# A two-layer hybrid decoder trunk on one core: four buffers of the expert stage at addresses of their own

## The reference

```python
def swiglu(h, w1, w3, w2):
    return (jax.nn.silu(h @ w1) * (h @ w3)) @ w2

def moe_swiglu(h, w_router, w1, w3, w2):
    logits = (h @ w_router).astype(jnp.float32)
    top_val, top_idx = lax.top_k(logits, TOP_K)
    probs = jax.nn.softmax(top_val, axis=-1)
    combine = jnp.sum(jax.nn.one_hot(top_idx, N_EXPERTS, dtype=jnp.float32) * probs[..., None], axis=-2)
    out = jnp.zeros_like(h)
    for e in range(N_EXPERTS):
        out = out + combine[..., e:e + 1] * swiglu(h, w1[e], w3[e], w2[e])
    return out
```

## Time and profile before

| quantity | value |
|---|---|
| median of 3 runs | 2164.58 us |
| the runs | 2161.36, 2164.58, 2164.84 us |
| the profiled execution's own time | 2164.58 us |
| its span, first to last instruction | 2162.6 us |
| TensorE matmuls busy | 2054.7 us, 95% |
| weight loads busy | 1752.7 us, 81% |
| VectorE busy | 1609.7 us, 74% |
| ScalarE busy | 1239.3 us, 57% |
| moved by DMA | 512.24 MB, mean 237 GB/s |
| mean granted TensorE clock | 0.981 |

### The profile page before, as it was taken

The page is one execution under the profiler, slowest core; times in us unless marked ns, Lnnn a source line. Parts: engine busy times, 40 slices in busy tenths (PEclk is TensorE's granted clock), DMA queues, the critical chain, the costliest instruction groups (busy, mean ns, idle before and its releaser), DMA issues.

```text
span 2162.6 us, 29146 instructions
## 1 busy us (share of the span) xinstructions
PE 2054.7 (95%) x10899; PEld 1752.7 (81%) x10899; DVE 1609.7 (74%) x1246; ACT 1239.3 (57%) x1015; POOL 6.7 (0%) x12
## 2 busy tenths in 40 slices
PE   7999999879998999999878999999999999999997
PEld 6997887769997988887767888888888888888886
DVE  5878855644544878955746889898888888888886
ACT  4544455334343554455434777777676777767774
POOL 0000000000000000000000000000000000000000
PEclk9999999989999999999988999999999999999999
DMA  8423454335554532455234999999999999999995
GB/s 274 156 79 98 144 187 156 104 100 181 188 186 135 176 98 80 141 172 191 78 126 164 376 349 355 350 352 376 329 375 334 370 350 355 375 329 375 335 376 199
DMA packets 239200, 512.24 MB, mean 237 GB/s; under 512 B 11391, under 2 KB 34039, under 8 KB 239132
## 3 DMA queue, kind: packets, MB, share of 16 engines
q1 hardware_dynamic: 238124, 507.60, 67.1%
q0 software_dynamic: 1008, 3.69, 0.5%
HBM read 510.19 MB, written 1.07 MB: 236 GB/s over the span
## 4 chain that ended last, share of the span: by engine, by line
PE 85%; DVE 9%; issue 3%; ACT 2%; DMA 0%; DVEq 0%; SPq 0%; ACTq 0%
PE PS L465 25%; PE PS L467 24%; PE PS L466 24%; PE PS L538 6%; DVE lo L1432 3%; PE PS L878 1%; PE PS L915 1%; ACT hi L1008 1%; PE PS L487 1%; PE PS L891 1%; PE PS L759 0%; DVE a_act L1533 0%; DVE x L1919 0%; DMA rows<-in_knorm_c 0%; DVE actT_lo L1506 0%
## 5 line engine op out<-in xcount | busy, mean ns | idle before, releaser
L1432 DVE TENSOR_TENSOR lo<-raw,hi 128x2048 fp32r<-128x2048 f32 x481 | 1095.1, 2290 | 327.9 <-ACT hi L1008 325.8
L1008 ACT ACTIVATE hi<-raw 128x2048 fp32r<-128x2048 f32 x481 | 920.2, 1916 | 470.6 <-PE PS L467 465.0
L465 PE MATMUL PS<-hi,e_hi 128*128 128x512 f32 x896 | 354.9, 396 | 1.4 <-DVE e_lo L1455 1.4
L467 PE MATMUL PS<-hi,e_lo 128*128 128x512 f32 x896 | 349.8, 390 | 0.0
L466 PE MATMUL PS<-lo,e_hi 128*128 128x512 f32 x896 | 349.4, 390 | 0.0
L465 PE MATMUL PS<-hi,actT_hi 128*128 128x512 f32 x640 | 255.8, 400 | 9.6 <-DVE actT_lo L1506 7.3
L467 PE MATMUL PS<-hi,actT_lo 128*128 128x512 f32 x640 | 251.0, 392 | 0.0
L466 PE MATMUL PS<-lo,actT_hi 128*128 128x512 f32 x640 | 250.8, 392 | 0.0
L465 PE MATMUL PS<-hi,fT_hi 128*128 128x512 f32 x536 | 209.7, 391 | 4.3 <-DVE lo L1432 2.4
L466 PE MATMUL PS<-lo,fT_hi 128*128 128x512 f32 x536 | 208.7, 389 | 0.0
L467 PE MATMUL PS<-hi,fT_lo 128*128 128x512 f32 x536 | 208.7, 389 | 0.0
(11 more groups left out here) (304 smaller groups left out, 2234.3 us busy)
## 6 DMA issues: line engine op xcount, KB each, us to landing
raw<-in_moe_w SPq DMA_DIRECT2D x336, 1024.0 KB, 5.2
raw<-in_w_in SPq DMA_DIRECT2D x92, 1024.0 KB, 5.2
raw<-in_ffn_w SPq DMA_DIRECT2D x33, 1024.0 KB, 5.3
raw<-in_w_br SPq DMA_DIRECT2D x12, 1024.0 KB, 5.1
raw<-in_w_out SPq DMA_DIRECT2D x8, 1024.0 KB, 5.0
hankel<-hankel_dram POOLq DMA_DIRECT2D x1, 1536.0 KB, 13.5
x<-in_x SPq DMA_DIRECT2D x2, 512.0 KB, 4.1
gain<-in_norm_mix POOLq DMA_DIRECT2D x2, 512.0 KB, 5.9
```

Source lines behind the costliest of these rows:

```text
L465: pe.matmul(out, a_hi, b_hi, start=first, stop=False, skip_group_check=True)
L467: return pe.matmul(out, a_lo, b_hi, start=False, stop=last, skip_group_check=True)
L1008: act.activation(hi[prog.u % SPLIT][:, :], raw[slot][:, :], COPY).then_inc(hi_made.sem, 1)
L1432: dve.tensor_tensor(lo[prog.u % RAW][:, :], raw[prog.u % RAW][:, :], hi[s][:, :].bitcast(F32), ALU.subtract).then_inc(lo_made.sem, 1)
```

## The change

`e_hi`, `e_lo`, `y_hi` and `y_lo` lose their `at` argument. They no longer lie over `actT_hi` and `actT_lo` but take the next free bytes behind `pickT`, 16,384 bytes per partition in all.

```diff
     pick = sb("pick", [P, TT, P])
     pick_r = sb("pick_r", [P, TT, P], F32R)
     pickT = sb("pickT", [P, TT, P], F32R)
-    e_hi = sb("e_hi", [P, KT, P], F32R, at=o0)
-    e_lo = sb("e_lo", [P, KT, P], F32R, at=o0 + 4096)
-    y_hi = sb("y_hi", [P, D], F32R, at=o0 + 8192)
-    y_lo = sb("y_lo", [P, D], F32R, at=o0 + 12288)
+    e_hi = sb("e_hi", [P, KT, P], F32R)
+    e_lo = sb("e_lo", [P, KT, P], F32R)
+    y_hi = sb("y_hi", [P, D], F32R)
+    y_lo = sb("y_lo", [P, D], F32R)
```

## The result

The changed kernel takes 2178.26 us in the median of four runs (2176.79 to 2179.85), the kernel before 2164.71 us (2161.36 to 2165.89) beside it. The ratio is 1.0065, with a 95% interval of 1.0048 to 1.0083. The forecast was 2164.6 us with a range up to 2169.0 us; the measured 13.6 us more lie outside it, on the side that had been given 4 in 100.

A forecast was written before the change was run, and what follows sets the result against it. TensorE's matmul stream was taken as the bound. The profiled execution's 2164.6 us (span 2162.6 plus 2.0) plus four terms of 0 gave 2164.6 us, range 2160.2 to 2169.0 us.

The forecast's parts named there:

- the side that had been given 4 in 100: Whole kernel: a slower outcome, chance 0.04, being 0.03 for the slower place plus 0.01 for drift.
- the second of the change's parts: e_hi and e_lo as stationary operands of 2688 expert matmuls: new place reads like the old, 0 us.
- the third part: y_hi and y_lo, moving side of 64 scatter matmuls: 7 ns between rows would move 0.4 us; taken as 0.
- The argument on cover: Expert matmuls of 227 ns hide their weight loads; a slower place must more than double the load's share to be felt.
- The bound "4 ns more, none of it hidden, is 10.8 us": Upper bound for e_hi and e_lo loads: 4 ns more on each of 2688 matmuls, 10.8 us.
- The first part: Waits on the four buffers' old and new places: none could go and none would come, 0 us.
- the writers: Copies and subtractions into the four buffers: 3 ns on all 48 is 0.1 us; term taken as 0.
- The rival of the slower place: e_hi and e_lo share a memory piece with streamed neighbours, slowing expert-stage loads: 10.8 us, 2175.4 us, chance 0.03.
- The tests that the prediction named: Expert stage: e_hi loads of 190 ns or more with matmuls over 228 ns apart show slower; 225 or less, faster.

The follow-up runs named there:

- the old region at the wrong offset: e_hi and e_lo over actT_hi again but 384 bytes further, y_hi and y_lo high, against the kernel before: 2177.69 us, ratio 1.0054.
- the fine probe's `st_a`: TensorE-alone kernel with finer stationary starts; this batch, 512 columns at equal starts, ran behind 128-column matmuls: 10.98 us, 228.8 ns a matmul.

## Why the prediction was wrong

The step that failed is the second of the change's parts, "I take 0, the value of the row nearest by kind". It inferred the new place from rows of others and ended in "So within a form the places read alike". The places were chosen by their distance, 82, 142 and 175 thousand bytes, and did read alike, but all of them, `e_hi`, `fT_hi`, `actT_hi`, `c_pT` and `attn`, are at 128 modulo 256. They differed in the coordinate that doesn't matter and agreed in the one that does. The experiments show in its place a matmul that slows down when the two starts differ modulo 256 bytes: 1.54 us per expert, 12.3 us in all, or 4.6 ns for each of the 2688 matmuls.

A row that spoke of it stood in the prediction, in the third part: matmuls on `y_hi` at 396 ns against 389 ns. I priced it (0.4 us) and did not ask for its cause, which is the same conflict in the other direction, a stream at 128 over `pickT` at 0. Priced on the 2688 matmuls instead of 64, those 7 ns would have been 18.8 us, the right order of size. That is a reading after the fact: the row alone doesn't say that the 7 ns come from the start, and with a difference of 64 a row on `y_hi` moved by 4 ns with equal starts.

The argument on cover failed as well. A load was to have "some 117 ns of cover", so that only a load twice as long could be felt. But the loads did not grow (188 ns before and after); what grew was the matmul that streams beside them, and it stands on the path with each nanosecond. The bound "4 ns more, none of it hidden, is 10.8 us" came near the measured loss by luck: its 4 ns were a difference between the loads of two forms, 188 and 192 ns, which has nothing to do with the 4.6 ns.

The first part held: no wait went and none came, and the writers kept their lengths. What bounds the kernel was also read rightly: with TensorE's stream the bound, a loss of 5 ns a matmul shows in full.

The rival of the slower place was the case that came true, at 2175.4 us against 2178.26 us measured, but its mechanism was not the right one. The neighbours have no part in it, as the old region at the wrong offset shows, and the distance has none either. I gave it 0.03 on the strength of rows that could not have shown it. The Trainium skill, page SBUF — State Buffer, section "Who interferes with whom", calls TensorE's two read ports, one for the moving operand and one for the weight load, independent of each other. The measurement differs and decides: with TensorE alone at work a float32r matmul over 512 columns takes 226.9 ns at equal starts and 233.3 ns at a difference of 64 bytes. What the prediction cited from that section, that engines meet only at the port pair of VectorE and GpSimd, is not tested here, since both operands are TensorE's own.

The tests that the prediction named worked in part: over 228 ns apart would show the slower place, and did; a median load of 190 ns or more, which it asked for besides, did not come. The stretches of the expert stage read 119.9 busy of 120 us, as good as unchanged: a slower stream keeps TensorE as busy as a fast one.

## What to carry to other kernels

If a kernel lives by matmuls over 512 columns with a fresh 128 x 128 float32r load each, give the stationary and the streamed buffer the same start modulo 256 bytes, and round the small tensors between them up to 256. A flag of 128 bytes ahead of them was enough to put four buffers off and cost 13.6 us. And when a change moves data without moving an instruction, compare the rows of before by residue of the address and not by distance: any two groups of the same instruction that differ in mean are a question to be answered before "same" is forecast.

## What the hardware showed unexpectedly

- The spacing of float32r matmuls over 512 columns with a load each depends on where the two operands start relative to each other, with a period of 256 bytes: 226.7 to 227.3 ns at equal starts, 229 to 234 ns at most unequal ones. Of the unequal ones 216, 240 and 252 bytes are as fast as equal starts (226.7 to 227.1 ns).
- It needs nobody but TensorE: it is there with all other engines idle and at a granted clock of 1.00, and the loads stay at 188 ns. It isn't there for bfloat16 (215.8 ns at 64 and 128 bytes, with loads of 98 ns) or for float32r over 256 columns at the one difference tried (119.8 ns equal, 118.5 ns at 128).
- The pace takes some ten matmuls to settle when the operands change. In the changed kernel's stretch above it is 231 ns for ten matmuls after the unequal pair has ended, then 226.7 ns; on the mean of all 56 down parts, the second to the ninth matmul are at 228.9 ns against 227.1 ns before. It happens without any unequal pair as well, as in the fine probe's `st_a` behind short matmuls and in the first nine matmuls of the up parts before the change. What buffer or queue does that was not tried, nor in which part of the reading the two operands meet.
